# Linear attention's weights picked by predicated copies; branch projections, their banks and their additions by token tile; linear attention's norm ahead of the first branch product

## The reference, cut to what matters

```
z = rms_norm(x, ln_mix) @ w_in            # 15 parts, among them g_q, g_k, g_v, g_r, merge
o_nsa = nsa_attention(...)                # branch 0
o_gla = gated_linear_attention(g_q, g_k, g_v, g_r, ...)       # branch 1
o_mem = memory_attention(m_q, mem, ...)   # branch 2
gates = sigmoid(merge + b_merge)
merged = gates[0] * (o_nsa @ w_branch[0]) + gates[1] * (o_gla @ w_branch[1]) + gates[2] * (o_mem @ w_branch[2])
x = x + merged @ w_out
```

```
attn = einsum('bhid,bhjd,bhijd->bhij', qb, kb, decay)         # decay is 0 above the diagonal
o = rms_norm(o, norm_g) ; return o * silu(r)
```

## Time and profile before

| | |
|---|---|
| median of 3 runs | 1996.36 us (1995.1 to 1997.03) |
| the profiled execution | 1997.19 us, its span 1995.5 us |
| PE busy | 1960.1 us, 98% of the span |
| POOL, ACT, DVE busy | 1593.1, 1045.1, 750.8 us |
| second block's mixers | about 1036 to 1304 us and 1526 to 1795 us of the span |

### The profile page before, as it was taken

How to read it: one execution, slowest core, us unless ns; L and a number is a source line. 1 busy time by engine, 2 the same in 40 slices (tenths; PEclk the granted TensorE clock), 3 DMA queues, 4 the chain that set the end, 5 groups by cost and what they waited for, 6 DMA issues and landing times.

```text
span 1995.5 us, 26511 instructions
## 1 busy us (share of the span) xinstructions
PE 1960.1 (98%) x9698; PEld 1583.3 (79%) x9698; DVE 750.8 (38%) x1652; ACT 1045.1 (52%) x1748; POOL 1593.1 (80%) x1160
## 2 busy tenths in 40 slices
PE   9999999999999999999999999899999999999999
PEld 7888777888888877788887777788888777778887
DVE  4534444000300444400055688521115478742111
ACT  6445666444644566644475444654446554555443
POOL 7888876988788887698879577888888867788886
PEclk9999999999999999999999999999999999999999
DMA  6655434555665543456564333456547333345553
GB/s 234 232 206 179 159 117 157 186 186 188 211 218 190 174 157 125 166 196 240 190 253 148 117 116 127 138 182 222 208 169 274 127 127 117 119 136 195 184 186 131
DMA packets 98204, 348.63 MB, mean 175 GB/s; under 512 B 13436, under 2 KB 14108, under 8 KB 97820
## 3 DMA queue, kind: packets, MB, share of 16 engines
q1 hardware_dynamic: 97372, 345.80, 50.2%
q10 hardware_dynamic: 704, 1.14, 0.2%
HBM read 345.85 MB, written 1.05 MB: 174 GB/s over the span
## 4 chain that ended last, share of the span: by engine, by line
PE 93%; DVE 3%; POOL 2%; issue 1%; ACT 1%; DMA 0%; SPq 0%; DVEq 0%; ACTq 0%; POOLq 0%
PE psum L569 28%; PE psum L571 27%; PE psum L570 27%; PE psum L707 2%; POOL lo L542 2%; PE psum L750 1%; PE psum L637 1%; PE psum L760 1%; PE psum L982 1%; PE psum L773 1%; PE psum L740 1%; DVE big L2142 0%; PE psum L1136 0%; PE psum L837 0%; PE psum L796 0%
## 5 line engine op out<-in xcount | busy, mean ns | idle before, releaser
L542 POOL TENSOR_TENSOR lo<-raw,hi 128x256 fp32r<-128x256 f32 (+1 forms) x1156 | 1592.9, 1401 | 388.2 <-ACT hi L1270 359.6
L1270 ACT ACTIVATE hi<-raw 128x1024 fp32r<-128x1024 f32 x616 | 647.8, 1059 | 507.3 <-PE psum L571 482.8
L569 PE MATMUL psum<-hi,h_hi 128*128 128x512 f32 x1632 | 654.0, 401 | 2.3 <-POOL lo L542 2.1
L571 PE MATMUL psum<-hi,h_lo 128*128 128x512 f32 x1632 | 640.6, 393 | 0.0
L570 PE MATMUL psum<-lo,h_hi 128*128 128x512 f32 x1632 | 639.4, 392 | 0.0
L569 PEld LDWEIGHTS psum<-hi,h_hi 128*128 128x128 f32 x1632 | 308.7, 189 | 72.9 <-POOL lo L542 6.0
L571 PEld LDWEIGHTS psum<-hi,h_lo 128*128 128x128 f32 x1632 | 308.0, 189 | 66.2
L570 PEld LDWEIGHTS psum<-lo,h_hi 128*128 128x128 f32 x1632 | 308.6, 189 | 60.3
L1811 DVE SCALAR_TENSOR_TENSOR big<-psum,small,big 128x256 f32<-128x256 f32 (+1 forms) x120 | 61.1, 551 | 749.5 <-ACT big L1363 749.5
L569 PE MATMUL psum<-hi,y_hi 128*128 128x512 f32 x832 | 334.3, 402 | 8.4 <-DVE big L2262 4.9
L571 PE MATMUL psum<-hi,y_lo 128*128 128x512 f32 x832 | 325.5, 391 | 0.0
(11 more groups left out here) (265 smaller groups left out, 1396.1 us busy)
## 6 DMA issues: line engine op xcount, KB each, us to landing
raw<-in_stream SPq DMA_DIRECT2D x616, 512.0 KB, 3.3
big<-in_w SPq DMA_DIRECT2D x14, 512.0 KB, 6.9
big<-in_post SPq DMA_DIRECT2D x6, 512.0 KB, 5.3
special<-in_b_merge SPq DMA_DIRECT2D x2, 1536.0 KB, 8.1
memkv<-in_mem SPq DMA_DIRECT2D x2, 1024.0 KB, 5.7
big<-in_band SPq DMA_DIRECT2D x2, 768.0 KB, 4.8
x<-in_x SPq DMA_DIRECT2D x2, 512.0 KB, 5.0
special<-in_special SPq DMA_DIRECT2D x2, 512.0 KB, 4.4
```

The source lines that it names most:

```text
L542: t = pool.tensor_tensor(M.lo[:, slot, w], M.raw[:, slot, w], f32(M.hi[:, slot_hi, w]), ALU.subtract)
L569: pe.matmul(out, lhs_hi, rhs_hi, start=start, stop=False)
L571: return pe.matmul(out, lhs_lo, rhs_hi, start=False, stop=stop)
L1270: act.activation(M.hi[:, slot_hi, :], M.raw[:, slot, :], ACT.Copy).then_inc(sem["hi"], 1)
```

## The change

It has four parts. (1) The weights of linear attention are no longer multiplied by masks and added: a level's scores are copied from PSUM where its mask is not zero, one `copy_predicated` for each level, four in a step, into a tile that one memset a layer has cleared; each copy counts one on the semaphore `gread`, and `att` is gone. Levels 0 to 6 copy only the queries that can have a weight (64 of 128), the diagonal copies all 128. (2) Branches 2 and 0 take banks 2 and 3 for the first token tile and 0 and 1 for the second, so that only the second tile waits for the strip `gr`. (3) A new semaphore `rows` counts when the first tile of a branch's last piece is done; DVE multiplies that tile then, and the next branch's first tile waits for that alone. (4) Linear attention's norm stands earlier in the list: `gla[3]` behind the second row step of branch 2, `gla[4]` and `gla[5]` behind the third, `gla[6]` and `gla[7]` behind the first and the second of branch 0. ACT's load of the logarithm/exponential table moves from the branch product to behind the last gate.

```diff
-ROWS2 = {2: 0, 0: 0, 1: 4}
+ROWS2 = {2: (2, 0), 0: (2, 0), 1: (4, 6)}
...
-        ("rows", 2): ([nu[17], gu[1][4]], [nu[18]], [gla[3]], [gla[4]]),
-        ("rows", 0): ([gla[5]], [gla[6]], [gla[7]], none),
+        ("rows", 2): ([nu[17], gu[1][4]], [nu[18], gla[3]], [gla[4], gla[5]], none),
+        ("rows", 0): ([gla[6]], [gla[7]], none, none),
...
             if m:
-                pe.wait_ge(sem[second[0]], second[1])
+                second()
-            t = rows_tile(c, m, kt, a_hi, a_lo, bank, start, stop)
+            t = rows_tile(c, m, kt, a_hi, a_lo, banks, start, stop)
+            if stop and m == 0:
+                t.then_inc(sem["rows"], 1)
...
                 if b == 2 and i == 0:
-                    evicted(len(names) + 1)
                     evicted(len(names))
+                    second = lambda: evicted(len(names) + 1)
                 if b == 0 and i == 0:
-                    pe.wait_ge(sem["branch"], 4 * layer + 2)
+                    pe.wait_ge(sem["branch"], 4 * layer + 1)
+                    second = lambda: pe.wait_ge(sem["branch"], 4 * layer + 2)
...
-                    act.wait_ge(sem["att"], 4 * (layer + 1))
+                    act.wait_ge(sem["gread"], 32 * (layer + 1))
...
-            elif what == "branch":
-                if step[1:] == (2, 0):
+                if b == 1:
                     exp_and_ln()
...
-                dve.tensor_tensor(prod[:, :, 0:4, :], psum[:, 4:6, :].rearrange("p h (i q) -> p h i q", i=4), masks,
-                                  ALU.mult).then_inc(sem["gread"], 1)
-                dve.wait_ge(sem["gread"], nxt("gread"))
-                by_query = prod.rearrange("p h i q -> p h q i")
...
+                for i in range(4):
+                    level = 4 * part + i
+                    half, first = (LEVELS[1 + level],) * 2 if level < 7 else (P // 2, 0)
+                    queries = lambda a: a.rearrange("p h (n t) -> p h n t", t=2 * half)[:, :, :, first:]
...
+                    taken(dve.copy_predicated(queries(V.att_flat.rearrange("p (h q) -> p h q", h=2)), queries(mask),
+                                              queries(psum[:, 4:6, i * P:i * P + P])))
...
-                dve.wait_ge(sem["used"], piece["rows", b, 3] + 1)
+                if m:
+                    dve.wait_ge(sem["used"], piece["rows", b, 3] + 1)
+                else:
+                    dve.wait_ge(sem["rows"], nxt("rows"))
```

More of the change, by code:

```diff
@@ L214 @@
 SEMAPHORES = (
-    "hi", "lo", "used", "quarter",
+    "hi", "lo", "used", "rows", "quarter",
     "x_in0", "x_in1", "ident", "const", "rot", "pre1", "pre2", "par", "mem_in", "masks", "angles", "stored", "w1_0", "w1_1",
@@ L585, in strip_piece, with rows_tile @@
         t.then_inc(sem["used"], 1)
-    def rows_tile(c, m, kt, a_hi, a_lo, bank, start, stop):
+    def rows_tile(c, m, kt, a_hi, a_lo, banks, start, stop):
         slot, slot_hi = c % RING, c % RING_HI
@@ L591, in rows_tile, with rows, half_rows @@
             w = slice(i * 512, i * 512 + 512)
-            t = product(psum[:, bank + 2 * m + i, :], a_hi[:, kt, m * P:m * P + P], a_lo[:, kt, m * P:m * P + P],
+            t = product(psum[:, banks[m] + i, :], a_hi[:, kt, m * P:m * P + P], a_lo[:, kt, m * P:m * P + P],
                         hi[:, slot_hi, w], lo[:, slot, w], start, stop)
         return t
-    def rows(c, kt, a_hi, a_lo, bank, start, stop=False, second=None):
+    def rows(c, kt, a_hi, a_lo, banks, start, stop=False, second=lambda: None):
         pe.wait_ge(sem["lo"], c + 1)
         for m in range(MT):
-            if m and second:
-                pe.wait_ge(sem[second[0]], second[1])
-            t = rows_tile(c, m, kt, a_hi, a_lo, bank, start, stop)
+            if m:
[3 more added lines that the diff above has]
+                t.then_inc(sem["rows"], 1)
         t.then_inc(sem["used"], 1)
-    def half_rows(c, m, kt, a_hi, a_lo, bank, stop):
+    def half_rows(c, m, kt, a_hi, a_lo, banks, stop):
         if m == 0:
             pe.wait_ge(sem["lo"], c + 1)
-        t = rows_tile(c, m, kt, a_hi, a_lo, bank, False, stop)
+        t = rows_tile(c, m, kt, a_hi, a_lo, banks, False, stop)
         if m:
@@ L613, in half_rows, with last_rows @@
             t.then_inc(sem["f"], 1)
-    def last_rows(c, kts, a_hi, a_lo, bank, turn, ylo={}):
+    def last_rows(c, kts, a_hi, a_lo, banks, turn, ylo={}):
         for m in range(MT):
@@ L622, in last_rows @@
                     pe.wait_ge(sem["ylo"], ylo[i])
-                half_rows(c + i, m, kt, a_hi, a_lo, bank, i == len(kts) - 1)
+                half_rows(c + i, m, kt, a_hi, a_lo, banks, i == len(kts) - 1)
     def turned_tile(src, m, pairs, banks, ready, until):
@@ L713, in down @@
             for i in range(kts):
-                rows(c + i, (s - n0) % 2 * kts + i, y_hi, y_lo, 4, s == n0 and i == 0)
+                rows(c + i, (s - n0) % 2 * kts + i, y_hi, y_lo, (4, 6), s == n0 and i == 0)
         c += 4
@@ L730, in feed_forward @@
         order = [(strips - s) % 2 * kts + i for s in ((2, 1) if gated else (1,)) for i in range(kts)]
-        last_rows(c, order, y_hi, y_lo, 4, turn_next, {kts: n0 + strips} if gated else {})
+        last_rows(c, order, y_hi, y_lo, (4, 6), turn_next, {kts: n0 + strips} if gated else {})
         return c + 4
@@ L903, in mix1 @@
                 pe.wait_ge(sem["y1lo"], 7 * layer + Y1_EVENT[kt])
-                rows(c0 + 24 + i, kt, y_hi, y_lo, 0, i == 0, second=("z5", layer + 1) if i == 0 else None)
+                rows(c0 + 24 + i, kt, y_hi, y_lo, (0, 2), i == 0, second=lambda: pe.wait_ge(sem["z5"], layer + 1))
             elif what == "half":
@@ L1192, in mix2 @@
                 b, i = step[1:]
+                second = lambda: None
                 if b == 2 and i == 0:
[L1194 removed]
                     evicted(len(names))
+                    second = lambda: evicted(len(names) + 1)
                 if b == 0 and i == 0:
[L1197 removed]
+                    pe.wait_ge(sem["branch"], 4 * layer + 1)
+                    second = lambda: pe.wait_ge(sem["branch"], 4 * layer + 2)
                 if b == 1 and i == 0:
@@ L1202, in mix2 @@
                 pe.wait_ge(sem["y2lo"], 10 * layer + Y2_EVENT[kt])
-                rows(piece[step], kt, y_hi, y_lo, ROWS2[b], i == 0, i == 3)
+                rows(piece[step], kt, y_hi, y_lo, ROWS2[b], i == 0, i == 3, second)
             elif what == "last_branch":
@@ L1211, in mix2 @@
                 enter(V.merged, (0, 1, 2, 3), "merged", 4 * layer, c,
-                      lambda cc, m, j: rows_tile(cc, m, j, h_hi, h_lo, 4, j == 0, False), lambda j: j // 2)
+                      lambda cc, m, j: rows_tile(cc, m, j, h_hi, h_lo, (4, 6), j == 0, False), lambda j: j // 2)
                 pe.wait_ge(sem["xlo"], 8 * n["feats"])
-                last_rows(c + 4, range(4, KD), h_hi, h_lo, 4, turn_next)
+                last_rows(c + 4, range(4, KD), h_hi, h_lo, (4, 6), turn_next)
                 c += KD
@@ L2122, in decay, with taken @@
             dve.tensor_tensor(e, e, kb, ALU.mult).then_inc(sem["eb"], 1)
+        def taken(instruction):
+            instruction.then_inc(sem["gread"], 1)
+            dve.wait_ge(sem["gread"], nxt("gread"))
         def gla_unit(hp, t):
@@ L2131, in gla_unit @@
                 part = t % 2
-                prod = V.gla_prod.rearrange("p (h i q) -> p h i q", h=2, i=5)
-                masks = V.masks[:, 4 * part:4 * part + 4, :].unsqueeze(1).broadcast_to((P, 2, 4, P))
+                if hp == 0 and t == 0:
+                    own(dve.memset(V.att_flat, 0.0))
                 dve.wait_ge(sem["score"], nxt("score"))
```

19 lines of the change are left out of this document (8 added, 11 removed).

## The result

The changed kernel takes **1998.98 us** (median of 16 runs, 1998.06 to 2001.27), the kernel before 1996.05 us beside it (16 runs, 1992.92 to 1998.26): ratio 1.0016, 95% interval 1.001 to 1.0023. It is 2.9 us slower, with 37 us less work on DVE. The profiled execution took 2001.27 us, 4.1 us more than that of before; it is the slowest of its 16, so the trace shows somewhat more loss than the median.

The account below looks back on a forecast made before the run. PE, busy 98% of the span, was taken as the bound. Later restarts and a low clock, less what POOL takes back, gave +1.8 and +1.1 us for the two layers: 1996.36 + 2.9 = 1999.3 us, range 1995.4 to 2004.0.

Parts of the forecast that it names:

- The four copies, 1.8 us: On DVE, a step's four predicated copies take 1.8 us, 1.9 us less than the product and sums now.
- Rival C: Copies much slower, 6 us a step, so SiLU starts 2.2 us late and delays ACT's chain: 2005.3 us; chance 0.04.
- SiLU starts at 1247.3, when the strip ends: On ACT, SiLU's start is decided by the end of the strip `gr`, 0.8 us earlier than now.
- The first wait, 1.78 us, gone; branch 2 ends at 1263.4: PE's whole wait before branch 2's first row step goes; branch 2 ends at 1263.4 in place of 1265.2.
- ACT's chain, 18.3 us: ACT works without idling from 1247.3 for 18.3 us, so the norm's exponential ends at 1265.6.
- DVE's tail, 3.5 us: Behind the exponential, DVE's small steps (0.8), norm product (1.5) and branch 2's first product (1.2) take 3.5 us.
- Rival B: The norm's tail on DVE runs beside POOL, about 4.5 us, with the clock low for longer: 2003.2 us; chance 0.22.
- PE restarts 1.5 us later: Before branch 0, PE gets its banks at 1269.1 to 1269.2 instead of 1267.66, 1.5 us later.
- The clock, +1.5 us in the first layer, 0 in the second: Behind PE's 5.8 us idle before branch 0, a low clock adds 1.5 us; the second layer had it already.
- POOL takes back: PE's shorter wait for POOL near 1300 recovers part of the delay, leaving +1.8 us first layer, +1.1 us second.
- Nothing elsewhere: Everything behind depends on PE, and no gap there is long enough to swallow the delay.
- Rival A: Branch 2's products are not held up by the norm, so both PE waits go: 1993.3 us; chance 0.12.

Follow-up runs that it names:

- half-norm kernel: The changed kernel with `gla[3]` and `gla[4]` still in front, `gla[5]` and the table load back behind branch 2's products: 1991.85 us, ratio 0.9977.
- filled wait: The changed kernel with 18 extra matmuls of 512 columns, read by nobody, in PE's wait before branch 0: 1996.88 us, ratio 0.9997.
- earlier rounding: The changed kernel with DVE's products before the norm's second half, `gla[6]`/`gla[7]` one row step later, ACT rounding branch 0's last piece before the last gate: 1989.27 us.
- the norm alone in front: The kernel before with only linear attention's norm and the table load moved forward (part 4): 2005.75 us, ratio 1.0048.
- the banks alone: The kernel before with only the new banks of branches 2 and 0 (part 2): 1994.61 us, ratio 0.999.
- the change without the norm in front: The changed kernel with linear attention's norm and the table load back in their old places: 1991.4 us, ratio 0.9976.
- only DVE's queue: The changed kernel with DVE taking both products of branch 2 before its half of `gla[5]`, other engines' lists kept: 1991.62 us, ratio 0.9978.
- the same, POOL in whole pieces: The half-norm kernel with POOL taking a piece in one instruction, not four quarters, from branch 0's last piece on: 1997.67 us, ratio 1.0012.
- the turns later: The changed kernel with DVE's products before the norm's second half and `gla[6]`, `gla[7]` behind branch 0's second and third row step: 1992.37 us, ratio 0.9982.

## Why the prediction was right, and where its sizes were not

The forecast of 1999.3 us (+2.9) was right, and so was the mechanism: PE's first wait goes, DVE's products are held up by the norm, and the second wait becomes longer than both were. Term by term, starts with the 1.1 us of start-up taken off:

- *The four copies, 1.8 us.* Measured 1.75 us [the DVE timeline above]. Right. Rival C is out by that row.
- *SiLU starts at 1247.3, when the strip ends.* This step failed, by 1.1 us: the table load starts at 1247.26 - 1.09 = 1246.2, when the last copy ends. Only SiLU's own instruction needs the strip, and the load in front of it does not wait for it. The whole ACT chain is earlier by as much, and of the signs named in the prediction this one did not come: the load follows DVE, not PE.
- *The first wait, 1.78 us, gone; branch 2 ends at 1263.4.* Gone, and 1264.24 - 1.09 = 1263.2. Right.
- *ACT's chain, 18.3 us.* Measured 18.7 us, 0.3 of it a wait for PE. Right.
- *DVE's tail, 3.5 us.* From the exponential's end at 1265.97 to the first product's end (half of 2.35 us behind 1268.03) it is 3.2 us: 0.1 and 0.8 for the small steps, 1.2 for L2096 (I took 1.5), 1.2 for the product. Rival B needed 4.5 us. That POOL would be idle there is what held it down; the half-norm kernel, where POOL is busy, shows B's small steps and its 1.70 us.
- *PE restarts 1.5 us later.* 1269.30 - 1.09 - 1267.66 = 0.55 us. The 1.1 us of SiLU's load are the difference; the longer chain and the shorter tail cancel. In the second layer 1761.13 - 1758.42 less the 2.1 us by which PE was late before the mixer: 0.6 us.
- *The clock, +1.5 us in the first layer, 0 in the second.* Mis-sized by 0.9 and by 1.0 us, about as much as the restart, in the other direction. A row step at the full clock is half of 5.73 us; the one behind the wait took 5.28 us, +2.4 us. In the second it took 5.21 us, 2.3 us more than at full clock, where before the low clock had cost 1.3 us: +1.0. I had taken the cost from a low clock behind an idle of 2.45 us, and behind 5.06 us it lasts longer. The filled wait shows the term by itself: by PE's starts in its trace its two mixers are 2.5 and 2.3 us shorter than those of the changed kernel. Of these 4.8 us the medians show only 2.3; the two traces differ outside the mixers too, by 1.0 us the other way (next but one point).
- *POOL takes back.* In the first layer 0.55 + 2.4 = 2.95, less 0.4 from its shorter wait (1.18 to about 0.8 us): 2.6 us by the end of the mixer, and 2.6 is measured (1.8 expected). In the second, 0.6 + 1.0, and POOL's wait grew by 0.4 where I had it go: +1.9 measured, 1.1 expected. A reading of the trace, not tested by itself: POOL's pieces follow ACT's late roundings, with gaps of 1.64 and 3.29 us in the first layer and 1.64 and 3.14 us in the second.
- *Nothing elsewhere.* Wrong by 1.5 us, and in the kernel's favour. Between the mixers PE's delay fell from 3.7 to 2.1 us. The kernel before had a low clock there that this execution did not; first before, then after, one stretch each:

```profile
1588.00:1589.00 1.00, 1.00 (x4) 0.81 (x3) 0.93 (x3) 0.00 (x0) 1.00 (x3) 0.50 0.00 0
```

```profile
1591.00:1592.00 1.00, 1.00 (x6) 0.82 (x5) 0.93 (x3) 0.00 (x0) 1.00 (x2) 1.00 0.00 0
```

In the traces of the filled wait and of the earlier rounding nothing is given back there. A second such stretch stands near 1097, in the first of the two mixers and ahead of all that the change moves on PE. It is in the traces of before and after, but not in that of the norm alone in front, whose program is the same as before's up to there; first before, then the norm alone:

```profile
1097.00:1098.00 1.00, 1.00 (x4) 0.81 (x3) 0.97 (x2) 0.00 (x0) 1.00 (x2) 0.50 0.00 0
```

```profile
1097.00:1098.00 1.00, 1.00 (x6) 0.83 (x5) 0.93 (x3) 0.00 (x0) 1.00 (x3) 1.00 0.00 0
```

So that one comes and goes without any edit, and moves PE by 1.5 us. Whether the change has a part in the stretch at 1588 stays open. Either way a difference of 1.5 us between two traces or two medians need not come from the edit. The table sets beside the medians what PE's starts give for the ends of the mixers alone, both layers together, from just ahead of branch 2's first row step to behind the merged product (1247.88 to 1303.53 in the trace of before, and the same matmuls elsewhere).

| against the kernel before, us | median | mixers' ends, one trace |
|---|---|---|
| the change | +2.9 | +4.5 |
| the norm alone in front | +9.0 | +10.1 |
| the banks alone | -2.1 | -1.0 |
| the change without the norm in front | -5.3 | -4.4 |
| only DVE's queue | -4.6 | -2.0 |
| the wait filled | +0.7 | -0.3 |
| half the norm in front | -4.4 | -5.5 |
| the same, POOL in whole pieces | +1.4 | +2.6 |
| the turns later | -4.0 | -2.3 |
| an earlier rounding | -7.1 | -5.8 |

The order of the change, its norm and DVE's queue is the same in both columns; differences of 1 to 2 us between kernels near each other are not settled by either.

So the two profiles differ by 1.1 (start-up) + 2.6 - 1.5 + 1.9 = 4.1 us, as measured. The mixers cost 4.5 us where 2.9 were expected, and 1.5 us were given back outside them. Inside them the errors cancelled in part: the restart was 0.95 us a layer too late, the clock 0.9 and 1.0 us too small, and POOL was expected to swallow 0.8 us a layer more than it did. The forecast's closeness is partly luck.

Rival A (products not held up) fell with the 5.06 us wait, yet its price was near: with the products taken first, DVE's order gave -4.6 us, of which its trace has 2.0 at the mixers' ends, and A had -3.1. That it was no more is put down to POOL: behind the two waits that went stands one of 2.01 us for it at 1291.75, and starting POOL earlier gave more. Part 3 was not run by itself; the norm alone in front, without it, left PE idle for 6.19 us, with it for 5.06.

The GPSIMD Engine Reference of the Trainium skill, section 1 (Specifications), has DVE instructions with two SBUF inputs, or in a 2-port mode, contend with GpSimd. The runs agree and give a size: the same product takes 1.23 us with POOL idle and 1.70 beside it, and the small steps with two inputs take 0.17 us alone, up to 0.75 beside quarters and 2.26 beside whole pieces. The step with one input mostly stays at 0.17 us, but took 0.65 in the kernel before and in the half-norm kernel; in which mode it ran, no run shows. The page ScalarE: Activation LUTs of the Trainium skill, section What ACT_TABLE_LOAD costs, adds some 1.4 us of drain to each load. This trace differs: the load at 1264.22 is 1.28 us long and the logarithm starts at 1265.51. The measurement decides.

## What to carry to other kernels

Before a step is moved forward in a shared list, look at each engine's queue by itself: the step must have its inputs when it comes to the head, or all that stands behind it waits with it. Here ACT's half of the norm could stand in front and DVE's half could not; splitting the step turned +2.9 into -4.6 us. Price an idle PE with the clock behind it (5 us of idle cost some 2.4 us more a layer), and when the waits on one engine are gone, look for the supplier that is late next: here POOL, whose start hangs on where ACT rounds. When the effect sought is as small as what chance moves in a run, compare the stretch that the edit touches in the two traces, and not the times alone.

## What was not expected of the hardware

- A DVE step on 8 numbers can be held up for nearly as long as POOL's instruction: 0.17 us alone, up to 0.75 beside quarters, 2.26 us beside whole pieces, which take 2.3 to 2.4 us. Long POOL instructions are bad neighbours for chains of tiny DVE steps.
- ACT's table load started at 1247.26, when the last copy ended, 1.3 us ahead of its activation, and so hid the wait for the strip, whose last matmul starts at 1247.94.
- Behind 5.06 us of idle the clock stayed at 0.50 while PE worked for over 5 us; with 18 unread matmuls in the gap it did not fall there.
- A predicated copy from PSUM takes 0.34 us for 128 numbers (0.29 to 0.45) and 0.45 us for 256, in the mean, in place of the product and sum of the earlier trace rows.
